# Half columns in the inverses' products, and their order against the side products, in a hybrid decoder trunk

## What is computed

```python
h = x @ w_in                      # columns for mixer A, mixer B and the merge gates
fa_mix = fa + (prev - fa) * mu_shift
# mixer A: RWKV-7, 16 heads of 64
S = S * w_t + (S @ a_t) outer b_t + v_t outer k_t        # one token at a time
y = S @ r_t
# mixer B: block-compressed, selected and window attention, gated
m = sigmoid(g_A) * (o_A @ w_up_a) + sigmoid(g_B) * (o_B @ w_up_b)
x = LayerNorm(ALPHA * x + m @ w_out)
```

## Time and profile before

| | |
|---|---|
| median of 3 runs | 2196.01 us (2194.1 to 2196.52) |
| profiled execution, its own time | 2197.86 us |
| its span | 2196.2 us |
| TensorE matmuls (PE), busy | 2151.9 us, 98% |
| TensorE weight loads (PEld), busy | 1886.5 us, 86% |
| VectorE (DVE) | 1074.4 us, 49% |
| ScalarE (ACT) | 416.5 us, 19% |
| GpSimd (POOL) | 501.7 us, 23% |
| granted TensorE clock, mean share | 0.994 |

### The profile page before, as it was taken

The page is one execution under the profiler, slowest core; times in us unless marked ns, Lnnn a source line. Parts: engine busy times, 40 slices in busy tenths (PEclk is TensorE's granted clock), DMA queues, the critical chain, the costliest instruction groups (busy, mean ns, idle before and its releaser), DMA issues.

```text
span 2196.2 us, 48740 instructions
## 1 busy us (share of the span) xinstructions
PE 2151.9 (98%) x21490; PEld 1886.5 (86%) x21490; DVE 1074.4 (49%) x1754; ACT 416.5 (19%) x1169; POOL 501.7 (23%) x373
## 2 busy tenths in 40 slices
PE   9999999999999999999999999999999999999997
PEld 8999977777877679999899999777777876799996
DVE  3554344442834634774646442444428356347745
ACT  1111122222112611110211111122221125111002
POOL 3333300001111024333223332000011110243431
PEclk9999999999999999999999999999999999999999
DMA  7555332224642266454354453223246422655551
GB/s 278 185 164 166 122 136 99 99 99 164 246 154 78 77 210 212 157 179 161 120 182 156 170 173 128 97 97 101 98 164 217 153 90 77 218 193 173 164 174 69
DMA packets 88979, 329.50 MB, mean 150 GB/s; under 512 B 11904, under 2 KB 11920, under 8 KB 86464
## 3 DMA queue, kind: packets, MB, share of 16 engines
q1 hardware_dynamic: 74592, 268.60, 36.5%
q0 software_dynamic: 11872, 53.59, 6.8%
q10 hardware_dynamic: 2304, 4.20, 0.6%
HBM read 315.91 MB, written 18.82 MB: 152 GB/s over the span
## 4 chain that ended last, share of the span: by engine, by line
PE 89%; DVE 5%; DMA 4%; issue 1%; POOL 1%; ACT 0%; SPq 0%; DVEq 0%; POOLq 0%; ACTq 0%
PE PB L762 25%; PE PB L812 3%; PE PB L830 3%; PE PB L821 3%; PE PB L826 3%; PE PB L816 3%; PE PB L803 3%; PE PB L806 3%; PE PB L1217 3%; DMA WT<-in_w_all 2%; PE PB L886 1%; PE PB L968 1%; PE PB L1048 1%; PE PB L951 1%; PE PB L953 1%; PE PB L946 1%
## 5 line engine op out<-in xcount | busy, mean ns | idle before, releaser
L762 PE MATMUL PB<-XT,WT 128*128 128x264 f32 (+1 forms) x2816 | 697.1, 395 | 4.0 <-DMA WT<-in_w_all 3.2
L762 PEld LDWEIGHTS PB<-XT,WT 128*128 128x128 f32 (+1 forms) x2816 | 506.4, 189 | 110.8 <-issue 19.7
L1411 ACT ACTIVATE VT<-PB 128x132 f32<-128x132 f32 (+2 forms) x256 | 69.7, 282 | 510.3 <-PE PB L816 132.3
L1411 ACT ACTIVATE ARENA<-PB 128x512 f32<-128x512 f32 (+5 forms) x197 | 88.3, 474 | 319.5 <-PE PB L1080 84.2
L600 POOL DMA_DIRECT2D out<-in_c_win x16 | 8.1, 506 | 508.0 <-DVE ARENA L1965 508.0
L600 POOL DMA_DIRECT2D ARENA<-in_c_sel x64 | 40.0, 625 | 248.4 <-issue 248.4
L621 POOL TENSOR_TENSOR TOEP<-WT 128x1024 f32<-128x1024 f32 x20 | 47.2, 2359 | 183.4 <-PE PB L816 133.5
L621 POOL TENSOR_TENSOR TOEP<-H 128x1024 f32<-128x1024 f32 x20 | 48.2, 2408 | 139.2 <-PE PB L816 127.3
L812 PE MATMUL PB<-ARENA,TOEP 128*128 128x132 f32 x640 | 78.8, 276 | 1.1 <-POOL TOEP L624 1.0
L816 PE MATMUL PB<-ARENA,TOEP 128*128 128x132 f32 x640 | 78.5, 276 | 0.0
L821 PE MATMUL PB<-ARENA,TOEP 128*128 128x132 f32 x640 | 78.5, 276 | 0.0
(11 more groups left out here) (444 smaller groups left out, 4194.5 us busy)
## 6 DMA issues: line engine op xcount, KB each, us to landing
WT<-in_w_all SPq DMA_DIRECT2D x340, 512.0 KB, 4.5
H<-in_w_all SPq DMA_DIRECT2D x120, 512.0 KB, 4.5
KNVC<-in_w_all SPq DMA_DIRECT2D x40, 512.0 KB, 4.2
out<-in_c_win POOLq DMA_DIRECT2D x16, 512.0 KB, 4.1
ARENA<-in_c_cmp POOLq DMA_DIRECT2D x64, 128.0 KB, 5.4
ARENA<-in_c_sel POOLq DMA_DIRECT2D x64, 128.0 KB, 4.2
TOEP<-in_toep POOLq DMA_DIRECT2D x2, 2048.0 KB, 7.9
ARENA<-in_states POOLq DMA_DIRECT2D x4, 1024.0 KB, 10.9
```

The lines of the kernel that those rows point to most:

```text
L762: ins = mm(PB[rows, bank, 0:T], WT[:, s, k, 0:rows.stop - rows.start], x, start=start, stop=stop)
L1411: return act(out, in_, ACT.Copy)
```

## The change

It has four parts.

1. In levels 1 to 4, y and z are made for the columns that can be other than zero: at level j these are every second group of 2^j, 32 of 64. The functions `left` and `right` pick them, `packed_half` names the same columns where they lie side by side in PSUM. y writes 256 columns of bank 0. ScalarE spreads them into a buffer `YL` of its own for each level, full width, whose other columns stay zero. z has `XX` transposed and `YL`, both full width, as weights, with 32 moving columns. VectorE's addition goes over half of `XX`.
2. All y products of a level come first, and the mark for ScalarE behind them; the side products follow, with nothing between them and z (filling behind y of levels 1 to 4: 0 calls for 2, behind z: 2 for 3). `tokb` is copied after z of level 1.
3. GpSimd clears `YL` once a layer, after the last main pair: `VT` (three levels) and a piece of the arena (the fourth). It stands ahead of the load of `TOEP`.
4. The table of filling: the bound at `mixers` is 20 tiles for 22; behind `cbt` stand 3 calls for 7, behind `scores(1)` 4 for none (`sc1`). In calls, at each place: the quads have 48 less a layer, `mixers` 27 for 11, `gates` 58 for 26, the sum is 736 in both.

```diff
+EARLY = 20
-    BEHIND.update({f"y{level}": 2, f"z{level}": 3 if level < LEVELS else 4})
+    BEHIND.update({f"y{level}": 0 if level < LEVELS else 2, f"z{level}": 2 if level < LEVELS else 4})
-BEHIND_MIX.update({"cb": 8, "cbt": 7})
+BEHIND_MIX.update({"cb": 8, "cbt": 3, "sc1": 4})
-        m = upto[L, "mixers"] = first + FIRST["gb"] * KT
+        m = upto[L, "mixers"] = first + EARLY * KT
...
+        YL = [VT[:, j, :].rearrange("p (q n) -> p q n", n=C) for j in range(3)] + [take(P, 2 * NCH, C)]
...
+        def parts_of(a, j):
+            return a.rearrange("p (b two m) -> p b two m", two=2, m=2 ** j)
+        def left(a, j):
+            return parts_of(a, j)[:, :, 0, :]
+        def right(a, j):
+            return parts_of(a, j)[:, :, 1, :]
+        def packed_half(a, j):
+            return a.rearrange("p (b m) -> p b m", m=2 ** j)
...
+                po.wait_ge(*step("mp_a", L * MAINS + MAINS - 1, "om"))
+                nc.gpsimd.memset(flat(VT)[:, :], 0.0)
+                mark("yl_p", L, nc.gpsimd.memset(YL[3][:, :, :], 0.0), "zero")
                 dma(TOEP[:, :, :], toep, d_toep)
...
                             if j < LEVELS:
-                                ins = mm(PB[ra, 0, q * C:q * C + C], LM[oa, q, :], XX[oa, q, :], start=True, stop=True)
+                                ins = mm(packed_half(PB[ra, 0, q * 32:q * 32 + 32], j), LM[oa, q, :], left(XX[oa, q, :], j), start=True, stop=True)
...
-                            if j < LEVELS:
-                                ins = beside(j, q, ra)
                         mark("rw_t", it, ins, f"y{j}")
+                        if j < LEVELS:
+                            for q, ra in eight:
+                                beside(j, q, ra)
...
-                                    mm(PB[other(ra), 4, cols], XX[ra, 2 * NCH + q, :], YY[ra, q, :], start=True, stop=True)
+                                    mm(packed_half(PB[other(ra), 4, cols], j), XX[ra, 2 * NCH + q, :], left(YL[j - 1][ra, q, :], j), start=True, stop=True)
...
-                                    ins = mm(PB[ra, 5, cols], YY[ra, q, :], XX[ra, 2 * NCH + q, :], start=True, stop=True)
+                                    ins = mm(packed_half(PB[ra, 5, cols], j), YL[j - 1][ra, q, :], right(XX[ra, 2 * NCH + q, :], j), start=True, stop=True)
...
                 scores(1)
+                project(L, "sc1")
...
+                            sc.wait_ge(*step("yl_p", L, "zero"))
+                            y = left(YL[j - 1].rearrange("p q n -> p (q n)"), j)
+                            mark("rw_a", it, copy(y, packed_half(PB[:, 0, 0:256], j)), f"y{j}")
...
                         if j == 1:
+                            wait(("rw_t", "z1"))
                             mark("rw_a", it, copy(rows[:, 1], PB[:, 3, :]), "tokb")
...
-                            v(f"z{j}", tt(XX[:, :, :], XX[:, :, :], z, ALU.add))
+                            m, n = 2 ** j, 2 * NCH * C
+                            xs = ARENA[:, at_xx:at_xx + 2 * (n + m)].rearrange("p (a n) -> p a n", a=2)[:, :, 0:n]
+                            xs = xs.rearrange("p a (b two m) -> p a b two m", two=2, m=m)[:, :, :, 0, :]
+                            v(f"z{j}", tt(xs, xs, PB[:, 4:6, 0:256].rearrange("p a (b m) -> p a b m", m=m), ALU.add))
```

More of the change, by code:

```diff
@@ L125, in plan @@
             for name, n in BEHIND.items():
-                m = upto[L, hq, name] = min(m + n + (0 if name != "low" else 9 if hq == 0 else 2 * L), first + FIRST["gb"] * KT)
-        m = upto[L, "mixers"] = first + FIRST["gb"] * KT
+                m = upto[L, hq, name] = min(m + n + (0 if name != "low" else 9 if hq == 0 else 2 * L), first + EARLY * KT)
+        m = upto[L, "mixers"] = first + EARLY * KT
         for name, n in BEHIND_MIX.items():
@@ L271, in hybrid_trunk @@
         SV = take(P, 6, C)
+        YL = [VT[:, j, :].rearrange("p (q n) -> p q n", n=C) for j in range(3)] + [take(P, 2 * NCH, C)]
         used[0] = at_chunks
         G4 = take(P, 4 * NCH, 2, C)
+        at_xx = used[0]
         XX, YY, LM = take(P, 4 * NCH, C), take(P, 2 * NCH, C), take(P, 2 * NCH, C)
@@ L369, in hybrid_trunk @@
                             + " ".join(f"lm{j + 1} z{j}" for j in range(1, LEVELS)) + f" z{LEVELS} st " + " ".join(f"d{c} s{c}" for c in ch)))
+        steps("yl", DEPTH, p="zero")
         steps("mix", DEPTH, a="half tanh gates pick", t="v0 v1 v2 v3 gates pick", v="gl gate")
@@ L1101, in _ @@
                         for q in range(2 * NCH):
-                            cols = slice(q * C, q * C + C)
+                            cols = slice(q * 32, q * 32 + 32)
                             if j < LEVELS:
                                 for ra in both:
-                                    mm(PB[other(ra), 4, cols], XX[ra, 2 * NCH + q, :], YY[ra, q, :], start=True, stop=True)
+                                    mm(packed_half(PB[other(ra), 4, cols], j), XX[ra, 2 * NCH + q, :], left(YL[j - 1][ra, q, :], j), start=True, stop=True)
                             for ra in both:
                                 if j < LEVELS:
-                                    ins = mm(PB[ra, 5, cols], YY[ra, q, :], XX[ra, 2 * NCH + q, :], start=True, stop=True)
+                                    ins = mm(packed_half(PB[ra, 5, cols], j), YL[j - 1][ra, q, :], right(XX[ra, 2 * NCH + q, :], j), start=True, stop=True)
                                 else:
@@ L1527, in _ @@
                         wait(("rw_t", f"y{j}"))
-                        n = C if j < LEVELS else 32
-                        mark("rw_a", it, copy(YY[:, :, 0:n], PB[:, 0, :].rearrange("p (q n) -> p q n", n=C)[:, :, 0:n]), f"y{j}")
+                        if j < LEVELS:
+                            sc.wait_ge(*step("yl_p", L, "zero"))
+                            y = left(YL[j - 1].rearrange("p q n -> p (q n)"), j)
+                            mark("rw_a", it, copy(y, packed_half(PB[:, 0, 0:256], j)), f"y{j}")
+                        else:
+                            mark("rw_a", it, copy(YY[:, :, 0:32], PB[:, 0, :].rearrange("p (q n) -> p q n", n=C)[:, :, 0:32]), f"y{j}")
                         if j == 1:
+                            wait(("rw_t", "z1"))
                             mark("rw_a", it, copy(rows[:, 1], PB[:, 3, :]), "tokb")
@@ L1622, in _ @@
                 take_out(L, "cbt")
+                take_out(L, "sc1")
                 for u in range(UNITS):
```

## The result

| | before | after |
|---|---|---|
| median, us (12 and 11 runs, interleaved) | 2195.84 | 2201.49 |
| ratio of the two | | 1.0035, 95% interval 1.0020 to 1.0049 |
| profiled execution, us | 2197.86 | 2202.52 |
| its span, us | 2196.2 | 2200.8 |

The ratio is +7.7 us (4.4 to 10.8) on 2195.8; the two medians lie 5.7 us apart, which is inside that interval. The forecast was +10.3, 2206 (range 2194 to 2217). A twelfth run of the changed kernel (9396 us, granted clock 0.59) is left out.

A forecast was written before the change was run, and what follows sets the result against it. The prediction took TensorE, busy 98% of the span, as the bound. Quad levels with their filling run elsewhere +16.0 us, the sample recurrence's wait -2.1, scores -3.6: +10.3 in sum, 2206 us, range 2194 to 2217.

## What to carry to other kernels

Before you halve an operand, find out which of the two holds the tile: a small product here cost by the larger of its weight and moving columns, so half the moving columns beside full weights gained nothing. Products that sit on different tiles belong in turn in the program; to put one group behind the other to cover a copy cost 0.75 us a level here, where filling had covered the copy at no cost. And look for "issue" waits in dense stretches of short instructions: a block of code needs at least 2.2 us from its fetch, long instructions between the short ones give it more time, and whoever takes them out should put the stops into the sum.

## What the hardware showed beyond that

- A stop for code can have a price beyond its length: behind 1.47 us of standstill the clock was granted at 0.51 for 6.91 us, and the four levels with it took 4.84 us more than four without. It is not the rule: behind 1.58 us in the same trace the clock stayed at 1.00.
- A wait that is long fulfilled mostly adds no instruction: 64 of them added 8 to TensorE's program.
- Starts overtake across tiles, by five or six records at a change of group in these traces.
